# Paged attention steps moved between the halves of the prompt's attention, and a shared PSUM bank exchanged

## The reference

```python
z = rmsnorm(x) @ w_in                      # q latent | kv latent | rope key | u | v
q_abs, q_pe, c_kv, k_pe = ...              # low-rank queries and keys, rotated parts
s = (q_abs @ c_kv.T + q_pe @ k_pe.T) * ATTN_SCALE          # 8 heads
p = softmax(where(mask, s, NEG_INF))
o = (p @ c_kv) @ w_uv
# prompt: keys are the prompt's own 1024 tokens, causal
# samples: keys are 4096 cached positions, read by page_table from
#          cache_kv_latent / cache_k_rope, and the 4 new ones
g = u * (tril(W_s) @ v_norm + b)           # chunked gating
x = x + rmsnorm(concat(o, g) @ w_out)
x = x + rmsnorm(relu(rmsnorm(x) @ w_ff_up)**2 @ w_ff_down)
```

## Time and profile before

| | |
|---|---|
| median of 3 runs | 2710.16 us |
| profiled execution | 2707.71 us |
| its span, first to last instruction | 2705.9 us |
| mean granted TensorE clock | 0.990 |
| PE busy | 2611.9 us (97%) |
| DVE / ACT / POOL busy | 1133.2 / 658.6 / 778.9 us |

### The profile page before, as it was taken

One profiled execution on the slowest core, in us unless ns is written; L12 is line 12 of the kernel. 1 busy time (PEld: TensorE's weight loads), 2 busy tenths in 40 slices (PEclk: granted clock), 3 DMA queues, 4 the chain that ended last, 5 costly groups with the idle time before them and its releaser, 6 DMA issues.

```text
span 2705.9 us, 42299 instructions
## 1 busy us (share of the span) xinstructions
PE 2611.9 (97%) x17128; PEld 2362.7 (87%) x17128; DVE 1133.2 (42%) x1626; ACT 658.6 (24%) x1111; POOL 778.9 (29%) x367
## 2 busy tenths in 40 slices
PE   8999999999999999999999999999999999999996
PEld 6985666979999999999879866669799999999995
DVE  5556666264222222221764566652732123222226
ACT  3125555141100110010241255551411000100111
POOL 2331000303433443333214300003033334433441
PEclk9999999999999999999999999999999999999998
DMA  6114232221111111111231243313211111111113
GB/s 218 47 36 127 81 83 68 112 88 44 43 47 47 47 42 44 47 47 47 104 111 40 56 119 82 85 54 118 80 47 47 47 47 42 43 47 47 47 41 134
DMA packets 91491, 185.96 MB, mean 69 GB/s; under 512 B 29664, under 2 KB 42144, under 8 KB 91360
## 3 DMA queue, kind: packets, MB, share of 16 engines
q1 hardware_dynamic: 88656, 175.75, 20.2%
q0 software_dynamic: 2560, 8.39, 1.1%
q10 hardware_dynamic: 144, 0.00, 0.0%
HBM read 157.77 MB, written 23.11 MB: 67 GB/s over the span
## 4 chain that ended last, share of the span: by engine, by line
issue 47%; PE 30%; POOLq 10%; DVE 7%; ACT 3%; DVEq 1%; POOL 1%; DMA 0%; SPq 0%; ACTq 0%
POOLq L604 9%; PE psum L1647 9%; PE psum L1830 3%; PE psum L1856 3%; PE psum L1677 3%; PE psum L1842 2%; PE psum L1632 2%; PE psum L1877 2%; PE psum L1733 1%; ACT z L849 1%; DVE sacc L1095 1%; DVE z L1142 1%; PE psum L1890 1%; POOL wl L605 1%; PE psum L1909 1%
## 5 line engine op out<-in xcount | busy, mean ns | idle before, releaser
L603 POOL TENSOR_TENSOR wh<-raw,ones 128x1024 fp32r<-128x1024 f32 x152 | 292.0, 1921 | 1286.3 <-PE psum L1647 1094.5
L1647 PE MATMUL psum<-hh,wh 128*128 128x352 f32 x2064 | 448.1, 325 | 3.0 <-issue 2.6
L1647 PE MATMUL psum<-hh,wl 128*128 128x352 f32 x2064 | 444.8, 323 | 0.0
L1647 PE MATMUL psum<-hl,wh 128*128 128x352 f32 x2064 | 444.3, 323 | 0.0
L605 POOL TENSOR_TENSOR wl<-raw,wh 128x1024 fp32r<-128x1024 f32 x152 | 419.5, 2760 | 22.0
L997 ACT ACTIVATE z<-z 128x1056 f32<-128x1056 f32 x64 | 69.7, 1089 | 1224.8 <-DVE stat L1504 1200.4
L1647 PEld LDWEIGHTS psum<-hh,wh 128*128 128x128 f32 x2064 | 351.5, 189 | 6.4 <-issue 5.1
L1647 PEld LDWEIGHTS psum<-hh,wl 128*128 128x128 f32 x2064 | 354.3, 188 | 0.0
L1647 PEld LDWEIGHTS psum<-hl,wh 128*128 128x128 f32 x2064 | 350.4, 188 | 0.0
L1500 DVE SCALAR_TENSOR_TENSOR z<-psum,rinv 128x1056 f32<-128x1056 f32 x64 | 80.5, 1257 | 552.6 <-PE psum L1647 542.8
L1520 DVE TENSOR_TENSOR z<-psum,z 128x1056 f32<-128x1056 f32 x104 | 130.8, 1257 | 394.6 <-PE psum L1647 341.7
(11 more groups left out here) (237 smaller groups left out, 3600.7 us busy)
## 6 DMA issues: line engine op xcount, KB each, us to landing
raw<-wst SPq DMA_DIRECT2D x160, 512.0 KB, 3.3
z<-cache_c SPq DMA_DIRECT2D x352, 64.0 KB, 1.8
x<-x_spill SPq DMA_DIRECT2D x4, 4224.0 KB, 14.2
raw<-cache_c SPq DMA_DIRECT2D x160, 64.0 KB
x_spill<-x SPq DMA_DIRECT2D x2, 4224.0 KB, 13.4
x_spill<-x SPq DMA_DIRECT2D x6, 1408.0 KB, 5.2
x<-xT SPq DMA_DIRECT2D x8, 528.0 KB, 8.2
yT<-x SPq DMA_DIRECT2D x6, 704.0 KB, 3.3
```

Source lines behind the costliest of these rows:

```text
L603: pool.tensor_tensor(wh[:, s, :], raw[:, s, :], ones[:, 0:1].to_broadcast([P, TW]), ALU.mult)
L1647: ins = pe.matmul(bank3(u, g), w[:, s, o:o + P], m[:, k, cols(g)], start=(k == 0 and n == 0), stop=(k == kk - 1 and n == 2))
```

## The change

- PE: `step_turn(c - 1)` goes from the end of ph 3 into ph 0 of the next step, behind `turn_p(i, 0)` and the values of the job before. `step_values(c - 1)` goes from the end of ph 0 to the head of ph 2, behind `values`, and writes bank 7 instead of bank 6. `step_scores(c)`, which writes bank 7 too, therefore also waits for `do_free`. `values` of the odd jobs goes behind `turn_p(i, 0)`. `new_turn` goes from ph 1 to ph 2, `new_values` behind `step_scores`. The keys of pairs 2 and 3 come one half earlier.
- ACT and DVE follow: `step_pt(c - 1)` and `step_sum(c - 1)` in ph 0, `step_out(c - 1)` in ph 2 behind `normalise`, `new_out` behind `step_max`.
- Before the loop: `o_vs` is stored behind the first four of the eight query DMAs; the last query unit is taken behind `bias(7)`; both `low_w` go behind the first values; the keys of pair 1 come before values 6 and 7.

```diff
-K_AT = {19: (2, 0), 23: (2, 1), 35: (3, 0), 39: (3, 1)}
+K_AT = {18: (2, 0), 22: (2, 1), 34: (3, 0), 38: (3, 1)}
@@ sync
                     for h in range(4):
                         sp.dma_start(qs[h % 2][NOPE:KQ, 2 * a + h // 2, :], ...)
-                sp.wait_ge(vt_free.sem, at.value(vt_free, NB + 1))
-                sp.dma_start(o_vs[l], vn[0:NS, NB % 2, :]).then_inc(vs_out.sem, 16)
+                    if a == 0:
+                        sp.wait_ge(vt_free.sem, at.value(vt_free, NB + 1))
+                        sp.dma_start(o_vs[l], vn[0:NS, NB % 2, :]).then_inc(vs_out.sem, 16)
@@ scalar, loop
                     take_pt(i)
+                    if ph == 2 and c % CHUNKS == 0:
+                        if c == 0:
+                            act.wait_ge(outs.sem, at.value(outs, 64))
+                        new_pt(c // CHUNKS)
                     if ph == 0:
+                        if c > 0:
+                            step_pt(c - 1)
                         take_keys(c, 0)
                         take_keys(c, 1)
@@ vector, before the loop
-                    if t < UNITS_Q:
+                    if t < UNITS_Q - 1:
                         take_q(t)
                     bias(t)
+                    if t == UNITS_Q - 1:
+                        take_q(t)
...
-                    if t == 6:
-                        low_w(0, at.whole(w_hi, 1))
...
                 take_vals(3)
+                low_w(0, at.whole(w_hi, 1))
                 paged_ropes()
                 take_vals(5)
+                low_w(1, at.whole(w_hi, 2))
                 maxima(0)
                 maxima(1)
-                take_vals(7)
-                normalise(0)
                 take_key(1, 0)
                 take_key(1, 1)
+                normalise(0)
+                take_vals(7)
@@ vector, step_out
-                                             in1=ps[6][:, 0:P], ...).then_inc(do_free.sem, 1)
+                                             in1=ps[7][:, 0:P], ...).then_inc(do_free.sem, 1)
@@ vector, loop
                     if i + 1 < HALVES:
                         normalise(i + 1)
+                    if ph == 2 and c > 0:
+                        step_out(c - 1)
...
                     if ph == 0:
                         if c > 0:
-                            step_out(c - 1)
+                            step_sum(c - 1)
...
                     if ph == 2:
+                        step_max(c)
                         if c % CHUNKS == 0:
                             new_out(c // CHUNKS)
-                        step_max(c)
-                    if ph == 3:
-                        if i in K_AT and K_AT[i][1] == 1:
-                            more_keys(K_AT[i][0])
-                        step_sum(c)
+                    if i in K_AT and K_AT[i][1] == 1:
+                        more_keys(K_AT[i][0])
@@ tensor, step_scores
                     pe.wait_ge(dexp.sem, at.value(dexp, c + quad + 1))
+                    pe.wait_ge(do_free.sem, at.value(do_free))
@@ tensor, step_values
                     evicted(RING_AT["x", c])
-                    pe.wait_ge(o_new.sem, at.value(o_new))
+                    if c % CHUNKS == CHUNKS - 1 and c < STEPS - 1:
+                        pe.wait_ge(dexp.sem, at.value(dexp, (c // CHUNKS + 1) * (CHUNKS + 1) + 1))
                     pe.wait_ge(do_free.sem, at.value(do_free))
-                            ins = pe.matmul(ps[6][rows_of(b), 0:P], ...)
+                            ins = pe.matmul(ps[7][rows_of(b), 0:P], ...)
@@ tensor, loop
-                    if i % 2 == 0 and k > 0:
+                    if ph == 2:
                         values(k - 1)
+                        if c > 0:
+                            step_values(c - 1)
                     turn_p(i, 0)
+                    if ph == 0 and c > 0:
+                        values(k - 1)
+                        step_turn(c - 1)
+                    if ph == 2 and c % CHUNKS == 0:
+                        new_turn(c // CHUNKS)
                     if i + 2 < HALVES:
                         scores(i + 2, 0)
                     if big:
...
-                        if c > 0:
-                            step_values(c - 1)
...
                     if ph == 2:
                         step_scores(c)
+                        if c % CHUNKS == 0:
+                            new_values(c // CHUNKS)
+                    if i in K_AT:
+                        u, h = K_AT[i]
+                        keys_of(u, h, ring(("k", u, h))).then_inc(t_full.sem, 1)
```

More of the change, by code:

```diff
@@ L83, in ring_table @@
         order.append((("p", i, 0), "act"))
+        if ph == 0 and c > 0:
+            order.append((("x", c - 1), "act"))
+        if ph == 2 and c % CHUNKS == 0:
+            order.append((("n", c // CHUNKS), "act"))
         if big:
@@ L89, in ring_table @@
             order += [(("d", c, 2), "dve"), (("d", c, 3), "act")]
-            if c % CHUNKS == 0:
-                order.append((("n", c // CHUNKS), "act"))
-        if ph == 3:
+        if ph == 2:
             if i in K_AT:
                 order.append((("k",) + K_AT[i], "act" if K_AT[i][1] == 0 else "dve"))
-            order.append((("x", c), "act"))
+        if ph == 3:
+            if c == STEPS - 1:
+                order.append((("x", c), "act"))
             if c == CHUNKS:
@@ L933, in _ @@
                             new_exp(c // CHUNKS)
-                            if c == 0:
-                                act.wait_ge(outs.sem, at.value(outs, 64))
-                            new_pt(c // CHUNKS)
+                    if i in K_AT and K_AT[i][1] == 0:
+                        more_keys(K_AT[i][0])
                     if ph == 3:
-                        if i in K_AT and K_AT[i][1] == 0:
-                            more_keys(K_AT[i][0])
                         step_exp(c)
-                        step_pt(c)
+                        if c == STEPS - 1:
+                            step_pt(c)
                         if c == CHUNKS:
@@ L1401, in step_out @@
                     dve.scalar_tensor_tensor(out=oacc[quad], in0=oacc[quad], scalar=stat[:, 6 + s:7 + s],
-                                             in1=ps[6][:, 0:P], op0=ALU.mult, op1=ALU.add).then_inc(do_free.sem, 1)
+                                             in1=ps[7][:, 0:P], op0=ALU.mult, op1=ALU.add).then_inc(do_free.sem, 1)
                     dve.drain()
@@ L1407, in step_out @@
                         dve.tensor_scalar(oacc[quad], oacc[quad], stat[:, 22:23], None, ALU.mult).then_inc(on_new.sem, 1)
+                        dve.drain()
                 gate_low(NB)
-                low_w(1, at.whole(w_hi, 2))
                 dve.wait_ge(vs_out.sem, at.value(vs_out, 16))
@@ L1915, in new_scores @@
                 def new_scores(quad):
+                    if quad == 0:
+                        pe.wait_ge(ct_free.sem, at.value(ct_free, 3))
+                        pe.wait_ge(qrd_new.sem, at.value(qrd_new, 1))
                     if quad:
@@ L1994, in _ @@
                         turn_keys(c, 2)
-                    if ph == 2:
-                        if c % CHUNKS == 0:
-                            new_values(c // CHUNKS)
                     if next_big:
@@ L2007, in _ @@
                         turn_keys(c, 3)
-                        if c % CHUNKS == 0:
-                            new_turn(c // CHUNKS)
                     if ph == 2:
                         step_scores(c)
+                        if c % CHUNKS == 0:
[3 more added lines that the diff above has]
+                        keys_of(u, h, ring(("k", u, h))).then_inc(t_full.sem, 1)
                     if ph == 3:
-                        if i in K_AT:
-                            u, h = K_AT[i]
-                            keys_of(u, h, ring(("k", u, h))).then_inc(t_full.sem, 1)
                         if c == STEPS - 1:
@@ L2022, in _ @@
                             out_part(0, (4, 5, 6, 7))
-                        step_turn(c)
+                            step_turn(c)
                         if c == CHUNKS:
```

29 lines of the change are left out of this document (14 added, 15 removed).

## The result

The kernel after took 2775.4 us (median of 6 runs) and the kernel before 2709.8 us beside it: ratio 1.0247, 95% interval [1.0232, 1.0263]. The profiled execution took 2773.8 us, span 2772.0. The direction and both new waits were as predicted; the loss is twice the predicted 34.6 us, and the time lies outside the range.

The account below looks back on a forecast made before the run. PE, busy 97% of the span, was taken to bound the kernel. The terms 5.7 + 17.7 - 3.4 - 1 - 1.7 = +17.3 us per layer, +34.6 for two, gave 2744 us; range 2722 to 2762.

Parts of the forecast that it names:

- (b): `step_scores` waits for `step_out`, which stands on DVE behind copy and normalisation, in steps 1 to 11: +17.7 us per layer.
- (a): `step_turn` leaves the end of ph 3; its 15.8 us wait is exchanged for `turn_p` waiting on `normalise`: +5.7 us per layer.
- (c): `new_turn` and `new_values` come long after their data, -3.4 us per layer; ring order covers page transpositions, -1.
- (d): Before the loop: two gaps shrink, until the page DMAs make the first `turn_keys` the bound: -1.7 us per layer.
- What bounds the kernel: PE is busy 97% of the span, no other engine over 42%, so whatever makes PE idle is paid in full.
- Steps 11 to 15 at 0: Moving `step_turn` changes little in these steps, one small wait for another: 0.
- Moving `step_values` ahead of this does not help: Putting `step_values` before the `step_scores` wait shifts PE and DVE's chain alike, since it starts at PE's own last transposition.
- 0 for the last pair: Steps 12 to 15: ph 2 is small, DVE has no copy, PE has long scores, so the `step_scores` wait adds 0.
- rival 2: No difference: only the wait of `step_scores` is empty, 5.7 - 3.4 - 1 - 1.7 = 0, 2710 us; chance 0.04.
- rival 4: Clock too: each step's waits bring a low stretch, 1.4 us for up to 22 steps, to 2775 us; chance 0.10.
- Rivals 1 and 2: Both new waits empty, 2676 us, chance 0.06; or only that of `step_scores` empty, 2710 us, chance 0.04.
- Rival 3: Half the loss: a step's two waits lend to each other, the second about 1 us shorter, 2723 to 2730; chance 0.17.

Follow-up runs that it names:

- e1: Kernel after with `step_out` issued on DVE ahead of the probabilities' copy and the normalisation in ph 2: 2738.9 us, ratio 1.0111.
- e5: Kernel after with `step_turn` back at the end of ph 3 and the odd jobs' `values` back ahead of `turn_p`: 2760.5 us, ratio 1.0192.
- e11: Kernel after with the edits of e1 and e5 together, `step_values` staying in ph 2: 2726.1 us, ratio 1.0065.
- e4: Kernel after with `step_values` and `step_out` put back to the end of ph 0, bank unchanged: 2727.2 us, ratio 1.0068.
- e9: Kernel after with the edits of e4 and e5 together, `step_values` and `step_turn` both back: 2712.3 us, ratio 1.0013.
- e14: e7 with only the new tokens' transposition moved to ph 2 and their values behind the paged scores: 2707.8 us, ratio 0.9996.
- e7: Kernel before with only the change's edits ahead of the loop, and two waits moved into `new_scores`: 2705.3 us, ratio 0.9990.
- e13: e7 with only the keys of pairs 2 and 3 one half earlier: 2706.8 us, ratio 0.9992.
- e6: Kernel after with the transpositions of new tokens and paged exponentials placed behind `turn_p(i, 1)`: 2780.6 us, ratio 1.0275.
- e3: Kernel after with the edits of e1 and e2 together: 2723.1 us, ratio 1.0051.
- e2: Kernel after with the head values and `step_turn` ahead of `turn_p(i, 0)` in ph 0: 2768.7 us, ratio 1.0220.
- e8: e4 with scores of half i+2 ahead of `turn_p` in ph 0 and the new tokens' transposition behind `turn_p(i, 1)`: 2713.4 us, ratio 1.0016.

## Why the prediction was right in kind and half in size

The terms of its sum, for two layers, and what the runs gave:

| term | predicted | measured | by |
|---|---|---|---|
| (b) `step_scores` behind `step_out` | +35.4 | +36.5 (and 34.4) | after - e1 (e5 - e11) |
| (a) `step_turn`'s wait exchanged | +11.4 | +14.9 (13.0 in the loops of the traces) | after - e5 |
| `step_values` at its new place, 7.5 of it lost cover in steps 12 to 15 | 0 | +11.6 (and 13.9) | e1 - e4 (e11 - e9) |
| (c) new tokens' pieces | -6.8 | +2.5 | e14 - e7 |
| (c) keys and ring | -2 | +1.5 | e13 - e7 |
| (d) ahead of the loop | -3.4 | -2.5 | e7 - before |
| sum | +34.6 | +64.5 | after - before: +65.6 |

- *What bounds the kernel* was right: PE's work is unchanged and its idle time was paid in full.
- *(b) was right in mechanism, place and size*: taking `step_out` out from behind the two DVE instructions gave back what was charged for it. Steps 4 and 8 were a little under-sized: in the second layer, where no low stretch lies in them, after less e1 is 1.50 and 2.15 us, for 1.19 and 2.0. `step_scores` waits 2.78 us in step 4 (at 304.08), but 1.27 of it stay in e1.
- *(a) was right in mechanism and 1.6 to 3.5 us short.* After less e5, its steps 0 to 3, 6, 7 and 10 are within 0.1 us of what it had (step 3 in the second layer, since a low stretch lies there in the first). Steps 5 and 9, behind the keys, cost 0.86, not 1.9, and steps 4 and 8 some 0, not -0.4; that the sum comes near owes something to luck, since the next miss offsets this one. "Steps 11 to 15 at 0" failed, 1.8 us a layer: there `step_turn` stands between `turn_p(i, 0)` and `turn_p(i, 1)`, and the latter waits 0.71 and 1.31 us for ACT (477.53 and 495.07).
- *The move of `step_values`, put at 0, is the largest miss.* The prediction had only "Moving `step_values` ahead of this does not help" and 0 for the last pair. I asked what the values would do where they went, and not what they had covered where they stood: 0.98 us of PE's work between the last copy of the first half and the first transposition of the second. The move cost 11.6 to 13.9 us; 7.5 of them are shown to be this cover. Of the rest, step 1 and steps 8 and 9, with a low stretch in step 9, no run parts cover from clock.
- *(c) failed in sign.* Its -3.4 a layer was to take away two waits. That of `new_turn` did go (2.4 us), but that of `new_values` did not: in the kernel after its idle times are 0.80 us (at 236.13) and 1.26 (at 382.44), 2.1 a layer for 1.7 before. And it priced the pieces at their new place with 0. A third entry of the ring in a half with the largest exponentials waits for ACT, 2.84 us, whatever its order (e6). 9.3 us in all. The keys had the same flaw on a small scale, 3.5 us. Both together with the exchanged bank cost 7.0 us (e9 - e7), where one by one they cost 4.0; the medians don't settle this difference.
- *(d)* was right within the measurement. In the trace it gained more, 2.98 us instead of 1.7; the page loads did not become the bound.
- *Slips in the working that change nothing:* rival 2 adds up to -0.4, not 0, and 2742.3 + 2.5 is 2744.8.
- *The clock.* The loops of after have six stretches at the low level and those of before one. Five of the six, as windows:

```profile
231.70:235.10 3.40, 3.17 (x13) 1.18 (x14) 1.86 (x5) 0.36 (x3) 0.00 (x0) 0.54 0.47 147
303.40:306.80 3.40, 2.69 (x9) 0.73 (x10) 1.04 (x3) 0.00 (x0) 0.00 (x0) 0.53 0.39 101
378.60:382.00 3.40, 3.18 (x10) 0.73 (x10) 1.00 (x4) 0.00 (x0) 0.00 (x0) 0.52 0.39 119
1607.50:1610.90 3.40, 3.40 (x11) 0.70 (x10) 1.85 (x4) 0.56 (x2) 0.00 (x0) 0.50 0.47 131
...
1706.50:1709.90 3.40, 3.40 (x29) 3.07 (x31) 0.33 (x1) 0.67 (x2) 0.00 (x0) 0.50 0.13 36
```

The first three begin within 0.5 us of where waits of 2.84, 2.78 and 2.20 us end (at 231.93, 304.08 and 378.79 us). What one costs is measured: in e7's first layer step 5 has one that before has not, in the second layer it is the other way, and the step is 1.62 us longer and 1.61 shorter. Five more make at most 8 us, spread over the measured terms above (the medians contain them). In the prediction this was rival 4; it is a part of the miss, not its cause, 8 of 31 us. That the upper end of rival 4 is the measured 2775 is coincidence: it had falls in up to 22 steps. The Trainium skill ("TensorE: Matmul & The Clock Gate", Part 1: The HAM clock gate) has the clock fall where activity is lacking; by that rule the prediction should have charged the new waits. The traces agree with it in part: one low stretch where the two largest groups of waits were 18 us a layer, six where they are 40. But e6, whose same two groups are 38 us, has two, and most long waits bring none, as that of 2.77 us at 1680.77 in the kernel after.

- *Rivals 1 and 2* (DVE done early) are excluded by the waits themselves. *Rival 3* (the two waits lend to each other) fell with e1, e3 and e5: each gives its own share back.

Open: why a particular wait of the same length brings a low stretch in one layer and not in the other; the 4 to 6 us of the `step_values` term that are not parted; and single us of the terms. That the sum meets the total to 1 us is partly luck, since terms of different occasions can be off by 2.

## What to carry to other kernels

Price a moved instruction at both ends: the wait that it loses, what it will wait for at its new place, and what it covered at the old one; left unpriced here, they were 9.3 us (new tokens' pieces) and 11.6 us (`step_values`), of a miss of 31. Where engines work lists in order, ask of a wait not whether the other engine has room, but what stands ahead of the releasing instruction in its list; moving that one instruction gave back 36.5 of 66 us. And to cover a wait, put work there that needs neither the waited-for engine nor delays what that engine owes next: one piece of scores gave 12 us, one piece more took 17 back.

## What the runs showed of the hardware that I had not expected

- Steps of one kernel repeat across kernels to 0.01 us where nothing of theirs is changed, and most steps of the second layer repeat the first's. A single stretch of 3.4 us at the lower clock then shows as +1.6 us in one step.
- An edit moves such stretches: e7 has one at 300.70 us in the first layer where before ran at full clock, and lacks the one of the earlier trace rows at the same place of the second layer.

```profile
300.70:304.10 3.40, 3.40 (x29) 2.82 (x26) 0.58 (x3) 1.17 (x5) 0.00 (x0) 0.52 0.00 0
```

- In e2 a low stretch lasted 13.6 us, over 11.56 us of PE's work, in each layer, and in e3 as long a one in the first; e2, e5 and e8 have ones of 6.8 us in their loops. In before and after only those of 3.4 us are seen there.
